# Attention stages of a three-layer block: where the compressed scores' step, the gates' tangents, two gate products and a rotary step stand in each engine's order

## The chip, the cores and the metric

The kernel runs on one core of a Trainium2 chip. The metric is the device time of one execution in microseconds (us). The program keeps five engines in step with semaphores: TensorE (PE; its weight loads are PEld) multiplies and transposes into eight PSUM banks of 128 x 512 fp32, ScalarE (ACT) copies, casts and evaluates functions, VectorE (DVE) does element-wise work and reductions, GpSimd (POOL) issues the DMAs of small tensors and some element-wise steps, and SyncE (SP) issues the weight loads.

## The reference

One sequence of 512 tokens, width 1024, passes through a first block and then through two equal layers, all in fp32. The first block is a gated feed-forward, a mixer and a second feed-forward. Its mixer has neighbourhood attention (8 heads, on an 8 x 64 grid) and three groups of dilated banded attention (4 heads each); both results are multiplied by sigmoid gates and summed. Each of the two layers mixes three attentions:

```python
o_a = nsa_attention(...)        # compressed + selected + window, 8 heads, 2 kv groups
o_b = swa_sink_attention(...)   # sliding window with sinks
o_c = mla_attention(...)        # latent: q and k = plain part (64) + rotated part (32)
g_a, g_b, g_c = jnp.split(jax.nn.sigmoid(h @ w_branch_gate), 3, axis=-1)
merged = g_a * (o_a @ w_branch_a) + g_b * (o_b @ w_branch_b) + g_c * (o_c @ w_branch_c)
x = x + merged @ w_out
```

In the compressed part a query sees 31 block summaries per kv group (held as 32), takes a masked softmax over them and multiplies by its own gate:

```python
s = einsum(qc, k_cmp) * scale
p_cmp = masked_softmax(s, cmp_end <= tq)
o_cmp = einsum(p_cmp, v_cmp)
```

## The kernel before

`Plan` writes a list of steps once; then each engine's program (`tensor`, `scalar`, `vector`, `gpsimd`, `sync`) walks the same list and issues its own part of each step in that order. So the place of a step in the list is its place in every engine's queue, and an engine whose next instruction waits holds up all that stands behind it. A semaphore value stands for all earlier instructions of its kind on that engine.

**Weights and products.** Every product is `dense` (L270): for each 128-row chunk three matmuls (L1691 to L1693; high and low parts of weights and activations), 24 of 128 x 512 for a full product of 1024 rows. A weight unit of 512 KB is loaded by SP (L2342), cast to its high part by ACT (L1877), and the rest is formed by DVE (L2010). `unit` asks for the split of the unit two ahead.

**PSUM.** Two rings of four banks: `PB`, taken in turn, and `OB`, which gives the bank that was given back longest ago. A bank is handed on with the events that must come before its next use.

**Attention** is `attend` (L508). Its input is a list of slots, each of two batches (two banks), taken two slots at a time as a pair. Turn p of the loop does, in this order: `turn` of the old pair (PE transposes the normalised scores of its four batches, L1775, and ACT copies each bank back, L1937); what waits in `behind`; `score` of the first new slot (PE L1767; DVE adds the mask and takes the extreme, L2083; ACT exponentiates, L1929) and of the second; `value` of the old slots (L1789); `norm` of the first new slot (DVE L2098 to L2114), `done` of the old, `norm` of the second new slot; then `between`: the hooks `post` and `pre` of the new units and a list of fill work, which keeps PE busy while DVE and ACT finish the softmax. A turn takes all four banks of `PB`, so the scores behind it wait until ACT has copied the first two.

**Fill work** is products for the gates. `gates` (L630) makes a whole product of 24 matmuls, whose bank `roomy` (L638) picks; `quarters` (L641) makes the same in four pieces of 6. `tangent` (L659) follows: DVE multiplies the bank by the norm's factor and so frees it (L2160), ACT takes the Tanh (L1953), and POOL stores the tile to DRAM (L2312). It runs at once when the bank is of `PB`, and in `behind`, after the next turn, when it is of `OB`. While four output banks are out or still to be opened `roomy` gives `PB`.

**Where the stages stand.** Neighbourhood attention: four pairs, fill `[ga[0:2], ga[2:3], ga[3:4], ga[4:6], ga[6:7]]`, the last list in the closing turn, which has no new scores. Its value tiles `va` come back from DRAM (`value_scratch`). Dilated groups 1 and 2: one pair each, fill of 8 and 4 quarters, right after the projections of their q and k. Latent attention (both layers): six pairs, fill `[opened[0:1], None, opened[1:2], None, opened[2:3], opened[3:4], opened[4:5]]`. Before pairs 1 and 3, `pre` calls `heads_in(2, True)` and `heads_in(3, True)`, which make the queries and keys of two more heads: three products for even m (plain keys, plain queries, rotated queries), two for odd. For even m ACT first copies the rotated bank (L1966), DVE multiplies it by the cosines (L2215), and the bank is free after both; then ACT copies the halves of the two plain banks (four of L1969). In the closing turn `done` of two output banks has been put in `behind` (ACT L1923, DVE L2076 free the bank).

Compressed, selected and window attention (both layers): eleven pairs, all fill in quarters. `post` of pairs 0, 2 and 5 issues `cmp_score` for the next query tile as one step, behind the norms of both slots: PE transposes two blocks (L1844), DVE masks, takes the maximum, subtracts (L2273, L2276, L2278), ACT exponentiates (L1997), and DVE, which waits for that, sums, inverts, weighs and multiplies (L2280 to L2286).

## Time and profile before

| | |
|---|---|
| median of 3 runs | 3093.63 us (3093.18 to 3093.67) |
| profiled execution, its own time | 3091.7 us |
| its span (first to last instruction) | 3089.5 us |
| PE busy | 3020.2 us |
| DVE busy | 1672.6 us |
| ACT busy | 1203.5 us |
| mean granted PE clock | 0.996 of full speed |

The chain of work that ended last is 89% PE. The span is the time between the first and the last instruction of the core; what the execution's own time has over it is start and end. Busy times are of instructions only, so 3089.5 less the busy time of an engine is the time in which it had nothing running.

### The profile page before, as it was taken

The page shows a single profiled execution, that of the slowest core. Times are in us where ns is not written, and L with a number is a line of the kernel's source. Part 1 is how long each engine was busy: PE and PEld are TensorE (multiplying, and loading weights), DVE is VectorE, ACT ScalarE, POOL GpSimd, SP SyncE. Part 2 cuts the span into 40 slices and gives each one's busy share as a digit, 9 for nine tenths or more (in the row PEclk, how much of TensorE's full clock was granted, in tenths as well). Part 3 has the DMA queues.
Part 4 walks back from the last instruction along what each step waited for, and adds up shares of the span by engine and source line. Part 5 has one row for each costly group of instructions (what it writes and reads, how often), then busy time and mean ns, then how long its engine had stood idle before and what let it go on. Part 6 is the DMA issues. An engine that isn't in the chain of part 4 may idle for free.

```text
span 3089.5 us, 40035 instructions
## 1 busy us (share of the span) xinstructions
PE 3020.2 (98%) x15272; PEld 2478.8 (80%) x15272; DVE 1672.6 (54%) x3050; ACT 1203.5 (39%) x2238; POOL 286.5 (9%) x344
## 2 busy tenths in 40 slices
PE   8999999999999999999999999999999999999998
PEld 7888887888888888778778888888778778888887
DVE  6653364446565426556656555436556666555434
ACT  4322334443432224645553322224546553322223
POOL 0000110001100012011001100013111001100002
PEclk9999999999999999999999999999999999999999
DMA  5333373325233333225225332334223315322332
GB/s 170 113 96 114 108 144 119 103 86 179 95 100 99 96 108 111 73 101 167 73 63 183 97 96 96 96 98 151 87 95 117 127 49 184 103 96 96 102 97 95
DMA packets 105996, 338.15 MB, mean 109 GB/s; under 512 B 15360, under 2 KB 15888, under 8 KB 105680
## 3 DMA queue, kind: packets, MB, share of 16 engines
q1 hardware_dynamic: 84816, 272.45, 28.0%
q0 software_dynamic: 20992, 63.15, 7.0%
q8 instruction: 123, 2.02, 0.3%
q14 instruction: 65, 0.53, 0.1%
HBM read 299.24 MB, written 27.52 MB: 106 GB/s over the span
## 4 chain that ended last, share of the span: by engine, by line
PE 89%; ACT 3%; DVE 3%; issue 2%; DMA 2%; POOL 1%; SPq 0%; POOLq 0%; DVEq 0%; ACTq 0%
PE bk L1691 26%; PE bk L1693 25%; PE bk L1692 25%; PE bk L1767 3%; PE bk L1789 3%; PE bk L1775 1%; PE bk L1730 1%; PE bk L1732 1%; PE bk L1731 1%; ACT t L1929 1%; ACT t L1937 1%; ACT t L1877 1%; DMA t<-value_scratch 0%; DVE t L2160 0%; DVE t L2010 0%
## 5 line engine op out<-in xcount | busy, mean ns | idle before, releaser
L1691 PE MATMUL bk<-t,t 128*128 128x512 f32 x3784 | 1481.0, 391 | 25.1 <-DVE t L2010 13.8
L1693 PE MATMUL bk<-t,t 128*128 128x512 f32 x3784 | 1469.2, 388 | 0.0
L1692 PE MATMUL bk<-t,t 128*128 128x512 f32 x3784 | 1468.3, 388 | 0.0
L1691 PEld LDWEIGHTS bk<-t,t 128*128 128x128 f32 x3784 | 712.6, 188 | 182.1 <-issue 26.2
L1693 PEld LDWEIGHTS bk<-t,t 128*128 128x128 f32 x3784 | 712.5, 188 | 147.3
L1692 PEld LDWEIGHTS bk<-t,t 128*128 128x128 f32 x3784 | 713.1, 188 | 141.9
L2010 DVE TENSOR_TENSOR t<-t,t 128x1024 fp32r<-128x1024 f32 (+3 forms) x538 | 616.7, 1165 | 353.9 <-ACT t L1877 353.2
L1877 ACT CAST t<-t 128x1024 fp32r<-128x1024 f32 (+3 forms) x538 | 511.3, 979 | 217.1 <-PE bk L1693 109.5
L1920 ACT CAST t<-t 128x512 fp32r<-128x512 f32 x88 | 54.6, 621 | 433.7 <-DVE t L2070 433.7
L1929 ACT ACTIVATE t<-t,t 128x256 f32<-128x256 f32 (+3 forms) x336 | 173.1, 516 | 95.8 <-DVE t L2083 94.9
L2316 POOL TENSOR_TENSOR t<-t,t 128x512 f32<-128x512 f32 x58 | 78.3, 1349 | 1387.4 <-ACT t L1907 1387.3
L2067 DVE SCALAR_TENSOR_TENSOR t<-bk,t 128x512 f32<-128x512 f32 x88 | 60.6, 691 | 246.8 <-PE bk L1693 246.7
L2083 DVE CUSTOM_DVE_ANT_0 t<-bk,t 128x256 f32<-128x256 f32 (+3 forms) x272 | 110.2, 456 | 125.3 <-PE bk L1767 77.9
L1903 ACT ACTIVATE t<-t,t 128x512 fp32r<-128x512 f32 x72 | 51.0, 722 | 224.3 <-DVE t L2293 195.1
L1767 PE MATMUL bk<-t,t 64*128 64x256 f32 (+7 forms) x672 | 115.3, 421 | 20.5 <-ACT t L1937 18.4
L1917 ACT ACTIVATE t<-t 128x512 f32<-128x512 f32 x88 | 55.5, 632 | 189.8 <-DVE t L2061 189.8
L1937 ACT COPY t<-bk 128x512 f32<-128x512 f32 (+2 forms) x200 | 95.3, 558 | 64.6 <-PE bk L1775 63.9
L1767 PEld LDWEIGHTS bk<-t,t 64*128 64x128 f32 (+1 forms) x672 | 65.7, 190 | 54.2 <-ACT t L1937 39.2
L2312 POOL DMA_DIRECT2D gate_scratch<-t x64 | 35.3, 552 | 728.1 <-ACT t L1953 563.4
L1789 PEld LDWEIGHTS bk<-t,t 128*64 128x64 f32 x1456 | 79.2, 137 | 24.3 <-issue 23.6
L1775 PE MATMUL bk<-t,t 128*128 128x128 f32 x728 | 90.6, 273 | 5.3 <-ACT t L1969 4.5
L1775 PEld LDWEIGHTS bk<-t,t 128*128 128x128 f32 x728 | 82.0, 140 | 15.4 <-ACT t L1969 5.7
(173 smaller groups left out, 1997.6 us busy)
## 6 DMA issues: line engine op xcount, KB each, us to landing
t<-in_f_g SPq DMA_DIRECT2D x88, 512.0 KB, 4.4
t<-in_f_u SPq DMA_DIRECT2D x88, 512.0 KB, 3.6
t<-in_f_d SPq DMA_DIRECT2D x64, 512.0 KB, 4.3
t<-in_gate SPq DMA_DIRECT2D x48, 512.0 KB, 3.7
gate_scratch<-t POOLq DMA_DIRECT2D x64, 256.0 KB, 2.3
t<-gate_scratch POOLq DMA_DIRECT2D x64, 256.0 KB, 3.7
t<-in_f_d SPq DMA_DIRECT2D x32, 384.0 KB, 3.1
t<-in_wo SPq DMA_DIRECT2D x24, 512.0 KB, 3.7
```

What stands on the lines that cost most here:

```text
L1691: pe.matmul(o, wh, xh, start=start, stop=False)
L1692: pe.matmul(o, wh, xl, start=False, stop=False)
L1693: return pe.matmul(o, wl, xh, start=False, stop=stop)
L1767: ins = pe.matmul(b["bank"][:, w["at"]:w["at"] + w["w"]], w["q"], w["k"], start=True, stop=True)
L1775: ins = pe.transpose(b["bank"][:, j * 128:(j + 1) * 128], b["S"][:, j * 128:(j + 1) * 128], P.cn("ident"))
L1789: ins = pe.matmul(v["o"], v["v"][j], b["PT"][:, c:c + 128], start=j == 0 and not v["add"], stop=end, skip_group_check=v["add"])
L1877: e.then_inc(act.copy(P.spl[u % NSPL][:, 0, 0:n], P.raw[u % NRAW][:, 0:n]), "halves", ("hi", u))
L1929: e.then_inc(act.activation(S, S, ACT.Exp, bias=w["nm"], scale=-1.0, accum_out=w["sm"]), "exps", (n, "e", j, i))
L1937: e.then_inc(act.copy(b["PT"][:, 0:b["w"]], b["bank"][:, 0:b["w"]]), "acts", (n, "a", j))
L2010: e.then_inc(dve.tensor_tensor(lo, P.raw[u % NRAW][:, 0:n], hi.bitcast(F32), ALU.subtract), "rests", ("lo", u))
L2083: e.then_inc(dve.tensor_tensor_reduce(b["S"][:, c:c + k], b["bank"][:, c:c + k], w["table"], -w["scale"], w["init"], ALU.add, ALU.min, w[" ...
L2316: e.then_inc(pool.tensor_tensor(P.acc[:], P.acc[:], s["q"][:], ALU.add), "pools", (n, "p"))
```

## The change

- **Compressed scores in two steps.** `cmp_score` keeps PE's transposes, DVE's first three operations and ACT's exponential. It is issued by a new hook `later`, between the norm of the first and of the second new slot. The four DVE operations behind the exponential become the step `cmp_share`, issued by `post` where all of it was before.
- **Tangents.** A gate product in `PB` inside `attend` still has its bank multiplied and freed at once; its Tanh and its store go to `behind`, so they follow the copies of the next turn.
- **Closing turn.** A flag `closing` makes `roomy` give `PB` in the closing turn. In latent attention this moves the fifth gate product from `OB` to `PB`.
- **Neighbourhood fill** becomes `[ga[0:3], ga[3:4], ga[4:5], ga[5:6], ga[6:7]]`: one product moves from turn 3 to turn 0.
- **Dilated groups 1 and 2.** A new argument `lead` issues the first quarter ahead of the first scores; the fill is then 7 and 4 quarters.
- **Latent heads.** In `heads_in(2, True)` the four copies of the plain banks come ahead of the rotated bank's copy and product.

```diff
@@ -172,6 +172,7 @@
         self.inside = False
+        self.closing = False
         self.unopened = 0
@@ -505,7 +506,7 @@
-    def attend(self, slots, fill=(), at_once=False):
+    def attend(self, slots, fill=(), at_once=False, lead=()):
@@ -513,6 +514,8 @@
         self.inside = True
+        for f in lead:
+            f()
@@ -579,17 +582,16 @@
+        def each(ss, name):
+            for s in ss:
+                for B in slots[s]:
+                    for U in B:
+                        if U.get(name):
+                            U[name]()
+
         def between(ss):
-            for f in ss:
-                for B in slots[f]:
-                    for U in B:
-                        if U.get("post"):
-                            U["post"]()
-            for f in ss:
-                for B in slots[f]:
-                    for U in B:
-                        if U.get("pre"):
-                            U["pre"]()
+            each(ss, "post")
+            each(ss, "pre")
             for f in next(fill, None) or ():
@@ -603,7 +605,9 @@
             if not new:
+                self.closing = True
                 between(())
+                self.closing = False
             for s in new[0:1]:
@@ -617,6 +621,7 @@
                 done(s)
+            each(new, "later")
             for s in new[1:2]:
@@ -636,14 +641,14 @@
     def roomy(self):
-        return self.OB if self.inside and len(self.OB.out) + self.unopened < 3 else self.PB
+        return self.OB if self.inside and not self.closing and len(self.OB.out) + self.unopened < 3 else self.PB
...
             if k == 0:
-                ring = self.roomy()
-                assert ring is self.OB
+                ring = self.OB
+                assert len(ring.out) < 3
                 b, bank, bt = ring.take()
@@ -657,16 +662,23 @@
     def tangent(self, name, m, ring, b, bank, tok):
-        def tangent():
+        def left():
             i, s, f = self.tmp.take()
...
             ring.give(b, (n, "g"))
-            self.gate_at[name, m] = (len(self.gate_at), self.load(self.D["gates"][len(self.gate_at)], s[:], (n, "t")))
-            self.tmp.give(i, self.gate_at[name, m][1])
+
+            def turned():
+                k = self.step("tangent", s=s, t=(n, "g"))
+                self.gate_at[name, m] = (len(self.gate_at), self.load(self.D["gates"][len(self.gate_at)], s[:], (k, "t")))
+                self.tmp.give(i, self.gate_at[name, m][1])
+            if self.inside and ring is self.PB:
+                self.behind.append(turned)
+            else:
+                turned()
         if ring is self.OB:
-            self.behind.append(tangent)
+            self.behind.append(left)
         else:
-            tangent()
+            left()
@@ -842,7 +854,7 @@
         self.unopened = 4
-        self.attend(self.batches(na_us), [ga[0:2], ga[2:3], ga[3:4], ga[4:6], ga[6:7]])
+        self.attend(self.batches(na_us), [ga[0:3], ga[3:4], ga[4:5], ga[5:6], ga[6:7]])
@@ -917,8 +929,8 @@
                     sms=dil_cols(S_SM, t, hh), rss=dil_cols(S_RS, t, hh), ot=lambda t=t, obk=obk: obk[t][2]))
-            self.attend(self.batches(us), self.portions(*[(gb[0:8], (3, 2, 2, 1)), (gb[8:20], (8, 4)),
-                                                          (gb[20:32], (8, 4))][g]), at_once=g > 0)
+            self.attend(self.batches(us), self.portions(*[(gb[0:8], (3, 2, 2, 1)), (gb[9:20], (7, 4)),
+                                                          (gb[21:32], (7, 4))][g]), at_once=g > 0, lead=[[], gb[8:9], gb[20:21]][g])
@@ -1231,7 +1243,7 @@
                     between()
-            if m % 2 == 0:
+            def turning():
                 places = to_place[m // 2] = []
@@ -1241,6 +1253,8 @@
                           done=rotated)
+            if m % 2 == 0 and not later:
+                turning()
             got = []
@@ -1251,6 +1265,8 @@
                 got.append((took, w))
+            if m % 2 == 0 and later:
+                turning()
             tq = got[1][0]
@@ -1492,6 +1508,11 @@
                         OB.give(b, (n, "b"))
+                        cmp_[qt] = (i, S, n)
+
+                    def cmp_shares(qt=qt):
+                        i, S, n = cmp_[qt]
+                        n = self.step("cmp_share", qt=qt, S=S, e=(n, "e"), sgs=sgs, sgt=sgt)
                         cmp_[qt] = (i, S, (n, "d"))
@@ -1514,14 +1535,18 @@
-                    def post(qt=qt, kind=kind, h=h, f_=cmp_scores, g_=cmp_turn):
+                    def post(qt=qt, kind=kind, h=h, f_=cmp_shares, g_=cmp_turn):
                         if h == 0 and kind == 0:
...
+                    def later(qt=qt, kind=kind, h=h, f_=cmp_scores):
+                        if h == 0 and kind == (qt > 0) and qt < 3:
+                            f_(qt + 1)
+
                     if qt == 0 and kind == 0 and h == 0:
-                        first_scores = cmp_scores
+                        first_scores = (cmp_scores, cmp_shares)
@@ -1540,10 +1565,11 @@
                                                        for j in range(qt + 1)],
-                        lambda: v_t, h, qt, 0.125, col, open=opn, post=post, done=done, most=4, add=True, gate=gate,
+                        lambda: v_t, h, qt, 0.125, col, open=opn, post=post, later=later, done=done, most=4, add=True, gate=gate,
                         sms=columns(S_SM, col, 1), rss=columns(S_RS, col, 1),
                         o=lambda qt=qt, h=h: half_out(obk[qt][1], h), ot=lambda qt=qt: obk[qt][2]))
-        first_scores()
+        for f in first_scores:
+            f()
         opened[14]()
@@ -1948,8 +1974,8 @@
                 e.then_inc(act.activation(a, a, ACT.Exp), "acts", (n, "a", g))
-        elif kind == "sigmoid":
-            e.wait_ge((n, "g"))
+        elif kind == "tangent":
+            e.wait_ge(s["t"])
             e.then_inc(act.activation(s["s"][:], s["s"][:], ACT.Tanh, scale=0.5), "acts", (n, "t"))
@@ -2267,8 +2293,7 @@
             mk = P.cn("cmpneg")[:, qt * 32:qt * 32 + 32].unsqueeze(1).broadcast_to([128, 8, 32])
-            some = P.cn("cmp01")[:, qt:qt + 1]
-            mx, sx = P.st[:, 168:176], P.st[:, 176:184]
+            mx = P.st[:, 168:176]
             e.wait_ge((n, "pe"), s["f"], P.c_tok)
@@ -2276,7 +2301,12 @@
             vec(dve.tensor_tensor(S3, S3, mx.unsqueeze(2).broadcast_to([128, 8, 32]), ALU.subtract), (n, "s"))
-            e.wait_ge((n, "e"))
+        elif kind == "cmp_share":
+            qt = s["qt"]
+            S3 = s["S"][:, 0:256].rearrange("p (h n) -> p h n", h=8)
+            some = P.cn("cmp01")[:, qt:qt + 1]
+            sx = P.st[:, 176:184]
+            e.wait_ge(s["e"])
             vec(dve.tensor_reduce(sx, S3, AX, ALU.add), (n, "1"))
```

## Rows read from the trace of the kernel before

**Rows 1.** The page, busy time of each engine: us, share of the span, instructions.

```profile
PE 3020.2 (98%) x15272; PEld 2478.8 (80%) x15272; DVE 1672.6 (54%) x3050; ACT 1203.5 (39%) x2238; POOL 286.5 (9%) x344
```

**Rows 2.** Waits of TensorE, whole span: us in total, times, longest us.

```profile
PE bk L1767 <- ACT t L1937: 18.4, 19, 3.2
...
PE bk L1691 <- ACT t L1923: 5.5, 2, 2.8
...
PE bk L1767 <- DVE t L2050: 1.5, 2, 0.7
```

**Rows 3.** The same view of 455:500, 1285:1318 and 1490:1560 us.

```profile
PE bk L1767 <- ACT t L1937: 2.3, 3, 0.8
...
PE bk L1767 <- ACT t L1937: 2.1, 3, 0.8
...
PE bk L1767 <- ACT t L1937: 5.4, 3, 3.2
```

**Rows 4.** Timeline, neighbourhood attention's first turn: start, length, idle before, releaser.

```profile
461.36 1.91 PE L1775 MATMUL bk<-t,t 128*128 128x128 f32 x16
464.02 2.11 PE L1767 MATMUL bk<-t,t 64*128 64x256 f32 x16 [0.75 <-ACT t L1937]
...
462.29 0.63 ACT L1953 ACTIVATE t<-t 128x512 f32<-128x512 f32 x1 [3.58 <-DVE t L2160]
```

**Rows 5.** Timeline, a turn with no tangent ahead of its copies.

```profile
1511.65 1.91 PE L1775 MATMUL bk<-t,t 128*128 128x128 f32 x16
1513.51 2.12 PE L1767 MATMUL bk<-t,t 64*128 64x256 f32 x16
...
1512.29 2.05 ACT L1937 COPY t<-bk 128x512 f32<-128x512 f32 x4 [1.72 <-PE bk L1775]
```

**Rows 6.** Timeline of TensorE, first value step of neighbourhood attention.

```profile
470.18 0.66 PE L1789 MATMUL bk<-t,t 128*64 128x128 f32 x8 [2.58 <-DMA t<-value_scratch]
```

**Rows 7.** Windows: length, busy time per engine, granted clock, DMA share, GB/s.

```profile
470.00:476.00 6.00, 5.83 (x24) 4.62 (x25) 2.73 (x8) 0.78 (x1) 0.00 (x0) 0.72 0.32 102
2198.00:2202.00 4.00, 3.95 (x10) 3.13 (x11) 1.69 (x1) 3.39 (x5) 1.28 (x1) 0.57 0.56 201
1499.70:1511.60 11.90, 11.89 (x84) 9.99 (x85) 7.30 (x30) 7.05 (x21) 0.54 (x1) 0.75 0.19 67
2452.40:2461.60 9.20, 9.19 (x84) 7.72 (x85) 7.33 (x30) 7.03 (x21) 0.54 (x1) 1.00 0.23 86
```

**Rows 8.** Timeline, latent attention's second turn, first such layer.

```profile
1276.54 0.63 PE L1775 MATMUL bk<-t,t 128*128 128x128 f32 x4 [1.39 <-ACT t L1969]
1277.78 1.06 PE L1775 MATMUL bk<-t,t 128*128 128x128 f32 x8 [0.60 <-ACT t L1969]
1278.92 2.94 PE L1767 MATMUL bk<-t,t 128*128 128x256 f32 x8
...
1272.53 0.61 ACT L1877 CAST t<-t 128x512 fp32r<-128x512 f32 x1
1274.76 0.58 ACT L1966 COPY t<-bk 128x512 f32<-128x512 f32 x1 [1.62 <-PE bk L1693]
1275.24 2.44 ACT L1969 ACTIVATE t<-bk 64x512 f32<-64x512 f32 x4
```

**Rows 9.** Timeline, compressed scores of the second query tile.

```profile
1494.64 1.91 PE L1775 MATMUL bk<-t,t 128*128 128x128 f32 x16
1499.71 2.93 PE L1767 MATMUL bk<-t,t 64*128 64x256 f32 x12 [3.16 <-ACT t L1937]
...
1493.47 0.69 DVE L2107 TENSOR_TENSOR t<-t,t 128x512 f32<-128x512 f32 x1
...
1495.76 0.41 DVE L2273 SCALAR_TENSOR_TENSOR t<-bk,t 128x256 f32<-128x256 f32 x1
...
1497.12 0.42 ACT L1997 ACTIVATE t<-t 128x256 f32<-128x256 f32 x1 [2.85 <-DVE t L2278]
...
1498.49 2.05 ACT L1937 COPY t<-bk 128x512 f32<-128x512 f32 x4
```

## The prediction

> **What bounds the kernel now.** I read the page first. TensorE is busy for 3020.2 of 3089.5 us [rows 1], so the kernel is a stream of matmuls with 69 us of holes, some 9 of them the start. No matmul is removed or added; the change can only close holes, open others, or move the clock. Then I read TensorE's waits. The largest group but the start is the scores (L1767) waiting for ACT's turn copies (L1937): 18.4 us in 19 pauses; then 5.5 us of gate products waiting for a bank that a split on ACT frees, and 1.5 us of scores waiting for a projected key [rows 2]. The same view by stage shows where: three pauses in neighbourhood attention (2.3 us), three in the later part of latent attention (2.1), three in compressed attention (5.4) [rows 3]. The two layers repeat each other's pauses, so a saving in the first is counted twice. Last I read the timeline around each pause, for what ACT did before its first copy, and the granted clock in windows.
>
> **The tangents.** At a turn TensorE transposes for 1.91 us. Where a `PB` gate product ends right ahead of it, ACT's next instruction is the Tanh, which must wait for DVE's product: it runs from 462.29 to 462.92, the copies follow, and the scores start 2.66 us after the turn (461.36 to 464.02), with 0.75 of idle time [rows 4]. Where no Tanh stands ahead, the first copy starts 0.64 us into the turn, four take 2.05, so the second is done some 1.7 us in, and the scores start 1.86 us after the turn with no pause [rows 5]. Moving the Tanh behind the copies makes the first case the second. That is worth all three pauses of neighbourhood attention, 2.3 us, and those of 1285 to 1318 us that have a Tanh ahead of them. There are three: 0.63, 0.73 and 0.75 by the timeline, 2.1 together [rows 3]. The 0.73 comes behind `heads_in(3)`, which is unchanged; two are left, 1.4 us, in each layer 1.4. What the Tanh now stands ahead of is the exponentials of the new scores. ACT has nothing then until DVE has read the scores, so one Tanh of 0.63 us is covered; three, behind the new first fill of neighbourhood attention, make 1.9 us, of which I take some 0.6 to delay the exponentials. The norms must be ready only after a further value step and a whole gate product, so this costs nothing; uncovered it would cost 0.6. The tiles in `tmp` and the stores go later by a turn, and nobody reads them before the merge.
>
> **The closing turn of latent attention.** The fifth gate product waits 2.77 us (5.5 in two times [rows 2]) because its `OB` bank is freed by a split that stands behind a Tanh and four copies on ACT. In `PB` it needs only the first copy, which now has no Tanh ahead. The first bank is copied while the turn still transposes [rows 5], so all 2.77 go, in each layer. The splits then run under the 24 matmuls. The bank is freed by DVE's product as before; the next stage needs it as its fourth.
>
> **One gate product moved to the first fill.** The value step waits 2.58 us for `value_scratch` [rows 6]. A gate product is 24 matmuls of the longest kind; at the mean of all PE instructions, 3020.2 / 15272 = 0.198 us [rows 1], they take at least 4.7 us, so with the 0.75 above gone TensorE comes to the value step 4.0 us later, behind the landing by 1.4. The moved split frees a weight buffer sooner, so a 512 KB weight load can run beside the value loads; it would have to delay them by more than 1.4 us to be seen. I take 2.58 in full; the bounds are 0 and 2.58. Turn 3 keeps one product as cover, as turns 1 and 2 have, and these have no pause for norms.
>
> **The clock.** After that pause the granted clock falls: 0.72 of full speed over the 6 us from 470 [rows 7], so (1 - 0.72) x 6 = 1.7 us lost between the 2.4 and the 1.2 GHz level. After the 3.16 us pause of compressed attention the same 84 PE instructions take 11.9 us at 0.75 in the first layer and 9.2 at 1.00 in the second [rows 7]: 2.7 us. I count both as given back, 4.4 together. The pause before 2198 us also has a fall behind it (0.57 over 4 us, 1.7 us) [rows 7]; that pause is in the initial `heads_in`, which is unchanged. The Trainium skill, "TensorE: Matmul & The Clock Gate", section "HAM oscillation — how this bites in real kernels", prices a fall as the throttled time x (1 - 1.2/2.4). By that rule the second fall, 11.9 us at a mean of 0.75, would cost 3.0 where the two layers differ by 2.7, and the whole sum would be 0.3 larger.
>
> **Compressed scores in halves.** Before, behind both norms, DVE runs three operations from 1495.76, ACT its exponential at 1497.12, then a cast, and only then the copies, at 1498.49, which the scores wait for until 1499.71 [rows 9]. The three DVE operations now start ahead of the second slot's norms. Those are two batches of some 1.05 us (the multiplication alone 0.69 [rows 9]) and the small copy of `cmp_turn`, 0.4, so ACT's exponential, cast and copies come 2.5 to 2.7 us sooner: copies from 1495.8, the second done by 1496.9. In turn DVE norms the second slot 1.3 us later (1495.76 to 1497.1 is what the three take), so the turn, which was all transposed at 1496.55, ends some 0.5 later. The scores start at about 1497.15 instead of 1499.71: 2.6 of 3.16. The bounds are 1.9 (the whole 1.3 is seen) and 3.16. At the other two places the pauses are 5.4 - 3.16 = 2.2 together [rows 3]. The turn starts there with the norms done long enough ahead, so I take 2.2 in full; bounds 0.9 and 2.2. Per layer 4.8. DVE's backlog then moves: the shares, a weight rest and a gate's product stand ahead of the next peaks, about 1 to 1.8 us late against TensorE. Covers are the waits of DVE for the value step that frees the score tiles, and the quarters of fill.
>
> **Latent heads.** The turn now waits 1.39 for the key bank and 0.60 for the query bank, whose copies ACT makes behind the rotated bank's; ACT itself stands idle for 1.62 us, until the third product is done [rows 8]. Put first, the four plain copies can start when the cast ends, at 1273.14, and end 2.44 later, at 1275.6; the rotated copy follows to 1276.15, and its product of 0.7 frees the bank at about 1276.9. The turn's last four transposes then end at 1277.4 and the scores start at about 1277.5 instead of 1278.92: 1.4. The bounds are 0.6 (just the order of one 0.58 us copy) and 2.0. The swap's DMAs start 0.9 us later on SP, and the next weight load behind them too; the rotated rows are wanted a turn later.
>
> **The lead quarter.** Six matmuls (at least 1.2 us by the same mean) fill the 0.73 us for which the scores wait for the key, twice: 1.5 [rows 2]. Its split moves ahead of the peaks on DVE, which costs them about 0.2; the first fill is 7 quarters instead of 8 and still longer than the softmax.
>
> **The sum.** Neighbourhood 2.3 + 2.6; lead 1.5; latent 2 x (1.4 + 2.8 + 1.4) = 11.2; compressed 2 x 4.8 = 9.6; clock 4.4. Together 31.6 us. The profiled execution took 3091.7, so 3060.1; the median of the runs is 1.9 above that execution, so 3093.6 - 31.6 = **3062**.
>
> **Rivals.**
> - *The backlog on DVE is seen.* The late norms of the second slot hold up the turn at each of the six places, by up to the three operations' 1.3 us, and the peaks behind them: 6 x 1.3 = 8 us back, 3070. For it: in compressed attention DVE has the shares, rests and norms in a row. Against: DVE is busy for 7.3 of 9.2 us there [rows 7].
> - *The clock falls elsewhere.* The 3.16 us pause is there in both layers and had a fall behind it in one only [rows 7]. The pause of the initial `heads_in` stays in both layers; one or two falls more, or none of the 4.4 given back, is 3064 to 3068. The skill's same page (section "What's actually happening") has the clock follow how busy the array has been lately, and its moment vary from run to run; by that a fall at 470 or 1500 is not sure to go, which is this rival.
> - *Half of it is not there.* The value loads land later with the weight load beside them, and the second halves of the exchange cost as much as they give: none of 2.6 + 1.7 at neighbourhood attention, 0.6 instead of 1.4 at the heads, 0.9 for 2.2: about 3071.
> - *Slower.* One mechanism: the first half of the scores, put between the norms, holds the turn so long that each of six places has a new 3.16 us pause, with 1.3 more and a fall of 2.7 behind it: 6 x 7.2 = 43, less the 13.5 that pauses and fall cost there already, is +29.7; the other stages save 19.3; net +10, 3104. It decides when a place costs above (19.3 + 13.5) / 6 = 5.5 us. The norms would have to be over 4 us late, and they are delayed by 1.3.
> - *No effect.* Each hole is followed by another wait of its own length; for that every one of five separate edits would have to fail.
>
> **Chances.** Forecast, 3058 to 3066: 0.62. DVE's backlog, to 3070: 0.13. Clock, to 3068: 0.12. Half, to 3074: 0.07. No effect 0.03, slower 0.02, still less than 3058: 0.01. The range that leaves out no more than 2 in 10 is 3058 to 3071. A change of 0.2% is 6.2 us, about what a measurement of this kernel can tell from none; faster by more has 0.95, within it 0.03, slower 0.02.
>
> **What would show it.** Right: scores behind L1937 wait under 5 us in all instead of 18.4; no wait for `value_scratch`; no L1691 wait for L1923; the key wait of L2050 gone; granted clock 1.00 near 475 and 1500. A wait of the turn (L1775) for DVE's norms in compressed attention would be the first rival, windows under 0.9 behind short pauses the second. Wrong by much: a pause of over 2 us at any place that had none, or peaks (L2083) so late that quarters end before the norms.

## The result, and the profile after

The changed kernel took 3057.69 us (median of 4 runs, 3057.0 to 3058.85), the kernel before 3093.4 beside it (4 runs, 3092.82 to 3093.67): a ratio of 0.9885, 95% interval 0.9868 to 0.9902, 35.7 us saved. The forecast was 3062 with a range of 3058 to 3071: the direction and the case were right, the gain was 4.1 us larger than the 31.6 of the sum, and the time lies 0.3 us below the range, on the side to which the forecast had given a chance of 0.01: all its rivals made the time longer. The profiled execution took 3057.74 us with a span of 3055.6. One execution of the kernel before, beside the experiments below, took 4685.77 us at a mean granted clock of 0.604, and no ratio or mean below counts it.

The page's row of TensorE's busy time, and its waits over the whole span (us in total, times, longest), which answer to [rows 1] and [rows 2]:

```profile
PE 3013.4 (99%) x15272; PEld 2474.4 (81%) x15272; DVE 1669.0 (55%) x3050; ACT 1204.0 (39%) x2238; POOL 289.1 (9%) x344
...
PE bk L1717 <- ACT t L1995: 3.6, 2, 1.8
...
PE bk L1793 <- ACT t L1963: 2.6, 6, 0.7
...
PE bk L1801 <- DVE t L2241: 1.5, 2, 0.8
...
PE bk L1801 <- DVE t L2319: 1.3, 2, 0.6
PE bk L1829 <- DVE t L2177: 1.0, 1, 1.0
```

The lines have moved: scores are L1793 (before L1767), the turn's transposes L1801 (L1775), their copies L1963 (L1937), dense matmuls L1717 to L1719 (L1691 to L1693), the tangent L1979 (L1953), a head's plain copies L1995 (L1969). The scores' wait for the copies fell from 18.4 us in 19 pauses to 2.6 in 6. The waits for the split (5.5), for the projected key (1.5) and for `value_scratch` (2.6) are not in the list any more. TensorE's pauses of 0.15 us and more were 60 with 60.3 us and are 41 with 33.0.

The windows behind the old pauses, and behind the one that stayed (the numbers behind the busy times are the granted clock, the DMA share and GB/s), to be held against [rows 7]:

```profile
470.00:476.00 6.00, 6.00 (x58) 4.88 (x55) 4.39 (x23) 6.00 (x22) 1.67 (x3) 1.00 0.53 195
1477.90:1489.40 11.50, 10.77 (x99) 8.82 (x98) 10.83 (x39) 9.46 (x31) 0.54 (x1) 1.00 0.21 70
2175.00:2179.00 4.00, 3.71 (x11) 2.96 (x12) 1.47 (x1) 3.61 (x6) 1.45 (x2) 0.64 0.65 201
2401.70:2413.20 11.50, 11.01 (x89) 8.51 (x78) 7.62 (x30) 6.46 (x22) 1.12 (x2) 1.00 0.31 103
```

The clock stays full at 470 us and in both compressed stages. Ahead of the final stores it fell in one place only, behind the 1.82 us pause of the initial `heads_in`, which the change leaves alone.

The timeline at neighbourhood attention's first turn (start, length, then idle time before and its releaser), to be held against [rows 4]:

```profile
467.85 1.91 PE L1801 MATMUL bk<-t,t 128*128 128x128 f32 x16
...
468.48 2.05 ACT L1963 COPY t<-bk 128x512 f32<-128x512 f32 x4 [9.93 <-PE bk L1801]
...
469.70 2.12 PE L1793 MATMUL bk<-t,t 64*128 64x256 f32 x16
470.39 1.70 ACT L1979 ACTIVATE t<-t 128x512 f32<-128x512 f32 x3
...
471.74 1.97 PE L1815 MATMUL bk<-t,t 128*64 128x128 f32 x32
...
471.96 0.53 ACT L1955 ACTIVATE t<-t,t 128x256 f32<-128x256 f32 x1
```

The copies start 0.63 us into the turn, and the scores 1.85 us behind it instead of 2.66, as forecast by [rows 5]. The three tangents stand behind the copies, and the first exponential starts where they end. The value step follows the scores without the 2.58 us of [rows 6].

Latent attention's closing turn:

```profile
1312.76 1.60 PE L1801 MATMUL bk<-t,t 128*128 128x128 f32 x12
1314.12 0.48 PE L1717 MATMUL bk<-t,t 128*128 128x512 f32 x1
...
1314.44 0.39 PE L1718 MATMUL bk<-t,t 128*128 128x512 f32 x1
...
1314.67 0.39 PE L1719 MATMUL bk<-t,t 128*128 128x512 f32 x1
...
1313.18 1.81 ACT L1963 COPY t<-bk 128x256 f32<-128x256 f32 x4 [3.47 <-PE bk L1801]
1314.89 1.08 ACT L1949 CAST t<-bk 128x512 fp32r<-128x512 f32 x2
```

The gate product (L1717) follows the transposes at once, and the split (L1949), which it waited for, runs under it. From the turn to the value step are 7.0 us (1312.76 to 1319.77) instead of 10.0 (1324.90 to 1334.91 in the kernel before).

Latent attention's second turn, to be held against [rows 8]:

```profile
1265.60 1.65 PE L1801 MATMUL bk<-t,t 128*128 128x128 f32 x12
1268.01 0.63 PE L1801 MATMUL bk<-t,t 128*128 128x128 f32 x4 [0.75 <-DVE t L2241]
1268.47 0.81 PE L1793 MATMUL bk<-t,t 128*128 128x256 f32 x3
...
1264.08 2.45 ACT L1995 ACTIVATE t<-bk 64x512 f32<-64x512 f32 x4
1266.55 0.59 ACT L1992 COPY t<-bk 128x512 f32<-128x512 f32 x1
```

One pause of 0.75 us stands in place of 1.39 and 0.60, and it is the one foretold: for DVE's product, which frees the rotated bank.

The compressed scores of the second query tile, to be held against [rows 9]:

```profile
1479.25 1.77 PE L1801 MATMUL bk<-t,t 128*128 128x128 f32 x12
1481.65 0.65 PE L1801 MATMUL bk<-t,t 128*128 128x128 f32 x4 [0.63 <-DVE t L2319]
1482.23 1.13 PE L1793 MATMUL bk<-t,t 64*128 64x256 f32 x8
...
1479.27 0.42 ACT L2023 ACTIVATE t<-t 128x256 f32<-128x256 f32 x1 [0.17 <-DVE t L2303]
1479.59 1.03 ACT L1903 CAST t<-t 128x1024 fp32r<-128x1024 f32 x1
1480.64 2.28 ACT L1963 COPY t<-bk 128x512 f32<-128x512 f32 x4
...
1480.57 0.69 DVE L2133 TENSOR_TENSOR t<-t,t 128x512 f32<-128x512 f32 x1
1481.17 0.42 DVE L2319 COPY t<-bk 128x256 f32<-128x256 f32 x1
```

From the turn to the scores are 2.98 us instead of 5.07. What is left is another wait than the one removed: the turn's last four transposes need the `PB` bank that `cmp_turn` holds, and DVE's small copy of it (L2319) now stands behind the second slot's norms (L2133).

### The profile page after: what moved, and what is told of

It reads as the page before. It is cut to its first block, busy times and chain, and to the rows that moved or that the text cites. A ratio compares the mean times of both kernels' runs of the same rounds, so it can differ in the third digit from the quotient of the medians.

```text
span 3055.6 us, 40040 instructions
## 1 busy us (share of the span) xinstructions
PE 3013.4 (99%) x15272; PEld 2474.4 (81%) x15272; DVE 1669.0 (55%) x3050; ACT 1204.0 (39%) x2238; POOL 289.1 (9%) x344
## 4 chain that ended last, share of the span: by engine, by line
PE 91%; ACT 3%; DVE 2%; issue 2%; DMA 1%; POOL 1%; SPq 0%; POOLq 0%; DVEq 0%; ACTq 0%
PE bk L1717 26%; PE bk L1719 26%; PE bk L1718 26%; PE bk L1793 3%; PE bk L1815 3%; PE bk L1801 2%; PE bk L1756 1%; PE bk L1757 1%; PE bk L1758 1%; ACT t L1955 1%; DVE t L2036 0%; ACT t L1903 0%; PE bk L1769 0%; DMA t<-gate_scratch 0%; ACT t L1995 0%
## 5 line engine op out<-in xcount | busy, mean ns | idle before, releaser
L1717 PE MATMUL bk<-t,t 128*128 128x512 f32 x3784 | 1480.2, 391 | 19.6 <-DVE t L2036 14.6
L1719 PE MATMUL bk<-t,t 128*128 128x512 f32 x3784 | 1468.6, 388 | 0.0
L1717 PEld LDWEIGHTS bk<-t,t 128*128 128x128 f32 x3784 | 712.3, 188 | 175.6 <-issue 26.9
L1719 PEld LDWEIGHTS bk<-t,t 128*128 128x128 f32 x3784 | 712.4, 188 | 146.9
L1963 ACT COPY t<-bk 128x512 f32<-128x512 f32 (+2 forms) x200 | 96.7, 559 | 103.1 <-PE bk L1801 102.0
L1793 PE MATMUL bk<-t,t 64*128 64x256 f32 (+7 forms) x672 | 112.7, 414 | 3.2 <-ACT t L1963 2.6
L1801 PE MATMUL bk<-t,t 128*128 128x128 f32 x728 | 91.4, 273 | 4.2 <-DVE t L2241 1.5
L1801 PEld LDWEIGHTS bk<-t,t 128*128 128x128 f32 x728 | 82.0, 140 | 15.1 <-issue 3.2
L1793 PEld LDWEIGHTS bk<-t,t 64*128 64x128 f32 (+1 forms) x672 | 64.1, 187 | 35.2 <-ACT t L1963 22.0
```

What stands on the lines that cost most here:

```text
L1717: pe.matmul(o, wh, xh, start=start, stop=False)
L1719: return pe.matmul(o, wl, xh, start=False, stop=stop)
L1793: ins = pe.matmul(b["bank"][:, w["at"]:w["at"] + w["w"]], w["q"], w["k"], start=True, stop=True)
L1801: ins = pe.transpose(b["bank"][:, j * 128:(j + 1) * 128], b["S"][:, j * 128:(j + 1) * 128], P.cn("ident"))
L1963: e.then_inc(act.copy(b["PT"][:, 0:b["w"]], b["bank"][:, 0:b["w"]]), "acts", (n, "a", j))
```

## The experiments

**How executions are compared.** The kernel before, run many times beside the experiments, took from 3088 to 3101 us (71 executions), more than most single edits are worth. A profile tells why. Windows of 2 us over the whole span give the granted clock in each; (1 - clock) x 2, summed over all windows but the last 16 us (the final stores), is the time lost to the clock. It comes in portions of 1.7 us, one or two behind a pause, and "remainder" below is the span less that. The places are the starts of these windows, "x2" a double portion. The sum counts the whole time of a fall, also what of it lies inside the pause: the double fall of 1498 began at 1498.81 and the scores at 1499.71, so it is priced 0.45 us too high (3.4 for 3.0).

| kernel | span | the clock fell at | lost | remainder |
|---|---|---|---|---|
| before | 3089.5 | 470, 1498 x2, 2198 | 6.8 | 3082.7 |
| before_again | 3089.2 | 1328, 1498, 2278, 2476 | 6.8 | 3082.4 |
| before_third | 3092.8 | 470, 1526, 2198, 2280 x2, 2454 | 10.3 | 3082.5 |
| changed | 3055.6 | 2176 | 1.7 | 3053.9 |
| after_again | 3053.8 | nowhere | 0 | 3053.8 |
| only_split | 3077.5 | 1328, 2270 x2 | 5.1 | 3072.4 |
| only_tangents | 3088.9 | 472, 706, 1328, 1498, 2226, 2276, 2448, 2474 | 13.7 | 3075.2 |
| only_closing | 3083.2 | 1246, 2222, 2444 | 5.1 | 3078.1 |
| only_fill | 3089.6 | 702, 1246, 1328 x2, 1502, 2228 | 10.2 | 3079.4 |
| only_lead | 3088.4 | 470, 1246, 1326, 2446 x2 | 8.5 | 3079.9 |
| only_heads | 3087.7 | 472, 1328, 1500, 2278, 2448 | 8.5 | 3079.2 |
| whole_at_later | 3090.7 | 472, 1332, 1502, 2450 | 6.8 | 3083.9 |
| key_ahead | 3051.9 | nowhere | 0 | 3051.9 |
| plain_ahead_all | 3049.7 | nowhere | 0 | 3049.7 |
| key_ahead_other_bank | 3050.4 | nowhere | 0 | 3050.4 |
| plain_other_bank | 3049.6 | nowhere | 0 | 3049.6 |

**before_again, before_third and after_again: is the spread the clock?** The two kernels, unchanged.

> The kernel before, unchanged, profiled once more. Theory (executions differ by the number of times that the granted clock falls to half behind a pause, and each fall takes 1.7 us; the schedule itself costs 3082.7 us in every execution, the 3089.5 of its profile less four times 1.7): the profile shows a number n of falls at places of about 472, 706, 1248, 1330, 1502, 2200 to 2228, 2278 and 2450, and the span is 3082.7 plus 1.7 n within 1 us, whatever n is. Rival (the executions differ by the length of the pauses themselves, a transfer that is now and then late): the span less 1.7 n is off by more than 2 us.

> The kernel before, unchanged, a third profile, for the same question: span 3082.7 plus 1.7 n within 1 us by the theory, with n likely 3 to 6 and not at the same places as in the other two.

> The changed kernel, unchanged, in more executions beside kernel before. Theory: its span is 3053.9 plus 1.7 n with n of 0 to 2, since only two or three places are left behind which the clock fell in any run, so its times spread over 3 to 4 us (3056 to 3060) where those of before spread over 9. Rival (the few falls of its first profile were chance): times up to 3065.

They took 3091.3 and 3094.93 us; windows of the first and then of the second:

```profile
470.00:476.00 6.00, 5.71 (x31) 4.69 (x31) 3.16 (x10) 1.24 (x3) 0.00 (x0) 1.00 0.29 93
1326.00:1332.00 6.00, 4.11 (x12) 3.33 (x13) 2.51 (x3) 2.50 (x5) 0.14 (x1) 0.76 0.28 93
...
2198.00:2202.00 4.00, 4.00 (x19) 3.29 (x18) 3.34 (x5) 3.76 (x6) 1.21 (x1) 1.00 0.44 144
```

```profile
1326.00:1332.00 6.00, 3.23 (x19) 2.48 (x18) 2.84 (x4) 4.06 (x8) 0.54 (x1) 1.00 0.20 79
...
2196.00:2202.00 6.00, 4.58 (x13) 3.64 (x14) 3.00 (x3) 4.88 (x9) 2.54 (x2) 0.72 0.42 134
2278.00:2286.00 8.00, 5.23 (x15) 4.05 (x15) 2.51 (x3) 3.87 (x8) 0.54 (x1) 0.66 0.30 99
```

The fall behind 470 us, on which the forecast counted, is missing in the first of them and one at 1326 is there instead; in the second it is the other way round, and behind 2278 there is a double one. The remainders of three profiles are 3082.7, 3082.4 and 3082.5, those of the changed kernel 3053.9 and 3053.8. So by these profiles the schedule's own gain is 28.7 us, and the rest of the difference between two executions is mostly the number of falls. The changed kernel's times in the repeat (median 3057.7, 3055.89 to 3058.91, 4 runs; ratio 0.9884, 0.9865 to 0.9902) stay within 3.0 us of each other, those of the kernel before within 13 (3088.08 to 3101.22, 7 runs). Both rivals fell.

A place at which the clock fell looks like this (before_again, TensorE's timeline; its window is the second one above):

```profile
1327.89 0.47 PE L1691 MATMUL bk<-t,t 128*128 128x512 f32 x1 [2.77 <-ACT t L1923]
```

**Each part alone.** Each of these is the kernel before with one part of the change's diff. only_split has `cmp_share`, `later` and what calls them; only_tangents the new `tangent`; the other four are

```diff
# only_closing (and the flag, set around the last `between`)
-        return self.OB if self.inside and len(self.OB.out) + self.unopened < 3 else self.PB
+        return self.OB if self.inside and not self.closing and len(self.OB.out) + self.unopened < 3 else self.PB
# only_fill
-[ga[0:2], ga[2:3], ga[3:4], ga[4:6], ga[6:7]]
+[ga[0:3], ga[3:4], ga[4:5], ga[5:6], ga[6:7]]
# only_lead (lines shortened)
-(gb[8:20], (8, 4)), (gb[20:32], (8, 4))
+(gb[9:20], (7, 4)), (gb[21:32], (7, 4)), lead=[[], gb[8:9], gb[20:21]][g]
# only_heads: the rotated copy behind the plain ones
+            if m % 2 == 0 and later:
+                turning()
```

> The kernel before with the compressed scores in two steps and nothing else. Theory (a pause costs its idle time plus the overlap that matmuls lose at a stop, some 0.1 us): per layer 3.16, 1.63 and 0.62 us of waiting for the turn copies shrink to one wait of about 0.6, 4.8 + 0.2 us, and the fall of the clock behind 1500 us goes, 2.7: 12 to 13 us less than before, about 3081. Rival (the clock falls elsewhere instead): 10 us, 3083.5, with a granted clock under 0.9 in some window where before had 1.00.

> The kernel before with the tangents of PB gates behind the next copies and nothing else. Theory: the turn-to-scores time falls from 2.66 to 1.86 us where a Tanh stood ahead. In neighbourhood attention the first 0.8 is given to the wait for value_scratch, which grows from 2.6 to 3.4; the two others give 1.6, the stage's end 0.6 to 1.1; in each layer 1.6 and some 0.6 of the closing turn's 2.77. Together 6.5 to 7.5 us, about 3086.5. Rival (the whole of every idle time and no more): 2.3 + 2 x 1.4 = 5.1 us, 3088.3.

> The kernel before with PB for the closing turn's gate and nothing else. The product now waits for the first turn copy, which still stands behind a Tanh: it starts 1.9 us into the turn plus 0.2 instead of 4.4, so each layer gives 2.3 to 2.6 us, 4.6 to 5.2 together, about 3088.5. Rival (the bank taken from PB is missed by the value step or the next stage): a new wait of the next products, under 3 us in all.

> The kernel before with the neighbourhood fill of 3, 1, 1, 1, 1 products and nothing else. Theory: the wait for value_scratch (2.58) goes whole and takes the clock's fall behind it along (1.7); with the overlap 4.3 to 4.7 us, about 3089. Rivals: the fall comes all the same, behind another pause, 2.7 us, 3090.7; or the weight load beside the value loads delays them, and a wait for value_scratch stays.

> The kernel before with the lead quarters of dilated groups 1 and 2 and nothing else. By the recorded sum 1.5 us (the 0.73 us waits of the scores for the key, twice). If a pause also costs the overlap of the matmuls around it, 1.9 to 2.1: 3091.4 against 3091.9.

> The kernel before with the plain copies ahead of the rotated one in the third head set, nothing else. Sum on record: 1.4 per layer, 2.8. With the overlap 3.0: about 3090.4. In the trace: waits of the turn for L1969 copies gone there, one of about 0.75 for the rotated bank's product in their place.

Against the kernel before on the same chips (medians 3093.76 for the first four, 3092.97 for the other two, from some 29 runs each), and with the remainder against the 3082.5 of the kernel before:

| kernel | median (runs) | ratio, 95% interval | remainder less by | the forecast's terms, without clock |
|---|---|---|---|---|
| only_split | 3079.70 (5) | 0.9960, 0.9948 to 0.9972 | 10.1 | 9.6 |
| only_tangents | 3087.11 (12) | 0.9980, 0.9971 to 0.9988 | 7.3 | 5.1 |
| only_closing | 3085.37 (11) | 0.9977, 0.9968 to 0.9985 | 4.4 | 5.5 |
| only_fill | 3090.73 (11) | 0.9991, 0.9982 to 0.9999 | 3.1 | 2.6 |
| only_lead | 3092.25 (12) | 0.9996, 0.9987 to 1.0004 | 2.6 | 1.5 |
| only_heads | 3092.53 (11) | 0.9997, 0.9989 to 1.0006 | 3.3 | 2.8 |

Five of the parts give what the sum's terms said within 1.1 us, where the waits ahead of the first matmuls alone differ by 0.5 to 1 us between executions; no part is worth nothing. only_tangents gives 2.2 more, as its expectation said (6.5 to 7.5): it also shortens each closing turn's pause, from 2.77 to 1.94 us, and the stage's end. The medians tell that badly: only_lead and only_heads save 2.6 and 3.3 us of schedule and 0.7 and 0.4 us of median, because falls take it back. only_fill came out at its rival's 3090.7 and not at the 3089 of its theory: the fall at 470 us was gone from its profile, and six portions at other places stood there instead.

Every execution, profiled or not, has its own mean granted clock, known to three digits. Span times this clock is a remainder with the falls in the final stores taken out too. Its mean is 3078.9 us for the 71 executions of the kernel before and 3048.7 for the eight of the changed kernel. Against the kernel before on their own chips the parts, in the table's order, come to 10.0, 7.5, 4.5, 2.4, 3.0 and 4.1 us less (standard errors of 0.3 to 0.8). The clock took 13.9 us from only_lead on average and 15.2 from only_heads, against 12.1 from the kernel before beside them.

The six remainders of the table add up to 30.8, the whole change's is 28.7. The parts share a pause, as the waits of only_tangents over the whole span show:

```profile
PE bk L1774 <- ACT t L1944: 13.5, 12, 3.2
...
PE bk L1796 <- DMA t<-value_scratch: 4.4, 1, 4.4
PE bk L1698 <- ACT t L1930: 3.9, 2, 1.9
```

The gate product's wait for the split (L1930) falls from 5.5 to 3.9 there, since the tangents' move shortens what stands ahead of that split; only_closing takes it away too. The value step waits 4.4 us instead of 2.6: the turn ends sooner and the values land a little later, so a pause closed ahead of that landing gives nothing until the moved product covers it. Of the 1.8 us more, 0.8 are the earlier turn; the landing itself moves from execution to execution, since in kernels that are alike up to there the wait was 2.2 to 3.4 us.

**whole_at_later: do the halves matter?** The compressed step at its new place, between the norms of the first and of the second new slot, but in one piece:

```diff
+            for s in new:
+                for B in slots[s]:
+                    for U in B:
+                        if U.get("later"):
+                            U["later"]()
# cmp_scores, unsplit, is called by "later" instead of "post"
```

> The kernel before with the compressed scores' step moved whole between the norms, not split: DVE waits there for ACT's exponential and runs the four last operations ahead of the second slot's norms, which come 3.2 us later than before instead of 1.3. Theory (both the place and the split count): the turn's last banks wait for the norms for about as long as the scores waited for the copies; 0 to 2 us less than before, 2.7 more if the clock keeps up. Rival (the place alone does it): as only_split, 12 us.

It took 3091.66 us (3087.28 to 3092.67, 11 runs), 0.9993 of the kernel before (0.9985 to 1.0002); its remainder is 1.4 us longer, 0.8 of it a longer wait for `value_scratch` (3.4 us for 2.6), and over all its runs the mean remainder is 0.2 us shorter. Its waits over the whole span, and its timeline at the first place:

```profile
PE bk L1774 <- ACT t L1944: 7.6, 13, 0.8
PE bk L1782 <- DVE t L2105: 7.4, 8, 2.0
```

```profile
1498.09 1.03 PE L1782 MATMUL bk<-t,t 128*128 128x128 f32 x8
1501.08 0.63 PE L1782 MATMUL bk<-t,t 128*128 128x128 f32 x4 [1.96 <-DVE t L2105]
```

The scores' wait for the copies is gone (18.4 to 7.6), and the turn's wait for the norms (L2105) has come in its place: DVE waits for the exponential and makes the four operations of the shares before it norms the second slot. This is the backlog rival's mechanism, and with the step in one piece it eats the whole gain. The halves are worth 3083.9 - 3072.4 = 11.5 us by the two profiles, and 9.8 by the means of all runs (10.0 less 0.2).

**What is left.** From the changed kernel, in `heads_in` with `later` unset: key_ahead makes the key's copies ahead of the rotated copy, plain_ahead_all all four plain ones; the bank's edit is

```diff
-                         b, bank2, bt = PB.take()
+                         b, bank2, bt = OB.take()
...
-                        PB.give(b, (n, "d"))
+                        OB.give(b, (n, "d"))
```

> All of the changed kernel, and in each head's step the key's two plain copies also stand ahead of the rotated copy on ScalarE. Theory (every pause on TensorE costs its length and the overlap of the matmuls around it, and the 1.82 us pause at 2175 us, or what is around it, brings the clock down): the pauses of 1.82 us in front of the dilated layers' scores shrink in both layers, about 1.9 us each, and the clock behind 2175 us stays at full, about 1.7 us more: 3052. Rival (the wait there is for the rotated rows, which come later by the two copies): the pause stays as a wait on VectorE, and the time is 3057 to 3059.

> All of the changed kernel, and all four plain copies ahead of the rotated one in the same step. Theory: the first pause closes, but the chain copy, product on VectorE, sum, placed rows starts about 2.4 us later and opens a pause of 1.5 to 2 us at the scores behind it, so 3056 to 3058, about the changed kernel's time. Rival (the placed rows have slack enough): 3052.

> The kernel of key_ahead, and the compressed step's turn takes its bank from the other pool, so that the next turn's last bank isn't held by it. Theory (the 0.63 us pause ahead of the compressed layer's first scores is for that bank's copy on VectorE): that pause closes, about 0.5 to 0.6 us in each of two layers, so 1 us below key_ahead: 3051. Rival (the other pool's bank is then late for a value product): same as key_ahead within 0.5 us.

> All four plain copies ahead, and the compressed step's turn in the other pool's bank. By adding what each gave in its own run (2.2 us less than key_ahead from the plain copies, 1.5 us less than key_ahead from the bank, both with the clock's falls taken out): a span of 3048.2 and a time of 3050.3, and no fall of the clock before the tail. Rival (the bank's 1.5 us came from elsewhere): 3051.8, as plain_ahead_all.

key_ahead took 3053.99 us (0.9868 of the kernel before, 0.9854 to 0.9883), plain_ahead_all 3051.84 (0.9864, 0.9847 to 0.9880), key_ahead_other_bank 3054.94 (0.9870, 0.9856 to 0.9885), each in 4 runs beside 3094.32; plain_other_bank 3051.82 (0.9867, 0.9846 to 0.9889) beside 3093.42. TensorE and ScalarE of plain_ahead_all around the place where the changed kernel had its 1.82 us pause:

```profile
1243.93 2.84 PE L1791 MATMUL bk<-t,t 128*128 128x128 f32 x12
...
1233.64 2.45 ACT L1993 ACTIVATE t<-bk 64x512 f32<-64x512 f32 x4
1236.11 0.59 ACT L1990 COPY t<-bk 128x512 f32<-128x512 f32 x1
```

The plain copies now run while ScalarE used to stand idle ahead of the rotated copy, the pause is closed, and the scores behind it (L1791) start without a wait (in the second layer after 0.43 us): my theory of a new pause of 1.5 to 2 us fell, its rival held. key_ahead left a wait of 0.93 us at those scores, for DVE's copies of rotated rows (L2254), so only half of the 1.9 us that I expected there came back. The other bank:

```profile
1477.50 1.76 PE L1801 MATMUL bk<-t,t 128*128 128x128 f32 x12
1479.65 0.63 PE L1801 MATMUL bk<-t,t 128*128 128x128 f32 x4 [0.39 <-DVE t L2133]
```

The turn's wait of 0.63 us becomes one of 0.39 for the norms themselves: about 0.25 us a layer, not the 0.5 to 0.6 that I expected. The remainders of single profiles hide part of what the bank is worth, since the first matmuls did not start alike: TensorE's 31st instruction came at 19.17 us in key_ahead and 18.83 in key_ahead_other_bank, at 19.05 in plain_ahead_all and 19.64 in plain_other_bank. From there to the last products the other bank saved 1.2 us in the first pair and 0.7 in the second, 0.5 of it at the two pauses; the rest is spread over small waits. The medians show nothing of it (3053.99 and 3054.94, 3051.84 and 3051.82). plain_ahead_all is, with plain_other_bank, the fastest that was run: 5.9 us less than the changed kernel, 4.2 of them by the remainders, and the rest is about one portion of the clock.

## Why the prediction was right on the pauses, and where it failed

By stage, from the start of the same matmul in the two profiles, with the clock's portions taken out:

| term | forecast | measured |
|---|---|---|
| neighbourhood: tangents and moved product | 4.9 | 6.2 |
| lead quarter | 1.5 | 2.0 |
| latent attention, each layer | 5.6 | 6.2, 6.2 |
| compressed attention, each layer | 4.8 | 4.2, 4.5 |
| clock, between the two profiles | 4.4 | 5.1 |
| clock, from profile to median | 0 | 1.8 |
| start and end of the execution | 0 | -0.7 |

The rows between and the rounding leave 0.2 of the 35.7 over.

- **The bound and the holes.** Right. TensorE was the stream with holes, each named pause closed, and no wait over 2 us came at a new place.
- **Tangents.** Right: 1.85 us from turn to scores, nothing lost at the exponentials or norms. Not counted in the forecast were two pauses at the end of neighbourhood attention (of 0.2 and 0.8 us, closed or shortened), 1.1 us: the term took the pauses of one window and stopped ahead of the stage's close.
- **Closing turn.** Right: 3.0 us for 2.77.
- **Heads.** Right: 1.5 us for 1.4, with the foretold pause.
- **Lead.** 2.0 for 1.5. A pause costs its listed idle time and the overlap of the matmuls on either side. In a stream without pauses a matmul of 0.39 us starts 0.23 us behind its forerunner (1314.44 and 1314.67 above), that is, before the forerunner's listed end; the listed idle time counts from that end. So each closed pause gave 0.05 to 0.25 us more than its row. That is most of latent attention's 0.6 a layer too.
- **Compressed.** 4.2 and 4.5 for 4.8: at the first place 2.1 of 3.16 came back and not 2.6, as I had DVE's small copy of `cmp_turn` in the sum of work ahead but not what is held until it is done, the turn's last bank. The 0.5 us for late norms, taken for the whole, came as this wait.
- **The clock.** This step failed. "I count both as given back, 4.4 together" took the falls of one execution for the kernel's own, and the sum then carried the 1.9 us between profile and median over as if the changed kernel had it too. Three profiles of the kernel before have falls at three different sets of places, 6.8, 6.8 and 10.3 us together. Its median time, 3093.4, less the 2.2 us between span and time and the 3082.5, leaves 8.7 us, five portions; the changed kernel's median leaves 3057.69 - 2.1 - 3053.9 = 1.7, one. So 7.0 us of the 35.7 are the clock's, where the forecast had 4.4, and the schedule's 28.7 stand against 27.2. These two, 2.6 and 1.5, are the miss. The 1.9 us was itself about one more portion of the clock. How the 35.7 divide is known only to some 1.5 us, though. By span times mean clock of all executions the schedule gave 30.2 and the clock 5.4, so that the clock's term is short by 1.0 and the schedule's by 3.0. One reason is the start: TensorE's 31st instruction came at 19.7 and 19.2 us in the two profiles of the changed kernel and at 18.6 to 19.1 in the three of the kernel before, ahead of everything that was changed, and the stages alone gave 29.3 (the table). By either reckoning both terms were too small, and the rest of the schedule's miss is the pauses and the overlap named above.
- **Rivals.** DVE's backlog is true of the unsplit step and not of the halves. "The clock falls elsewhere" was right as a mechanism and had the wrong sign here: it reckoned with fewer falls given back, never with more. "No effect" speaks of five separate edits; there are six. A fall moves between places from one execution to the next, but each of them stands behind a pause, and the long pauses are gone. The Trainium skill, "TensorE: Matmul & The Clock Gate", section "What's actually happening", says that the same kernel shows a different number of slow matmuls from run to run, which it says of a kernel's start; the traces show it in the middle of a kernel too (four, four and six portions). Its section "HAM oscillation — how this bites in real kernels" prices a fall at half of the throttled time. The remainders agree: with that price three profiles whose spans differ by 3.6 us come to within 0.3.

A count of pauses would have brought the clock's term nearer. Between start and end the kernel before has eleven pauses of over 1.3 us (those of 470, 1247, 1276, 1329, 1499, 1526 us and the second layer's five), and the changed kernel has two, of 1.82. The one profile that the forecast had lost four portions at eleven such pauses, and nine pauses fewer, at 4 / 11 of a portion each and 1.7 us a portion, are 5.6 us. The three profiles, two of them taken later, lost 14 portions at 33 such pauses, which makes it 6.5. Both are estimates; 7.0 or 5.4 were measured.

The length counts too. In the sixteen profiles together 30 of the 45 pauses of 1.9 us and more had a fall behind them, or beginning in them, 13 of the 59 between 1.3 and 1.9 us, one of the 18 between 0.95 and 1.3, and none of some 290 between 0.6 and 0.95. The change closed all five long ones. Five falls were double, and they are the five that began 0.7 to 1.1 us before their pause ended; of the 39 single ones the earliest began 0.64 us before that, and most began behind it.

Open: what decides at which of these pauses the clock falls in a given execution, and when. The shortest with a fall behind it had 1.11 us (only_tangents, at 706); the changed kernel's pause at 698 us has 1.0 and had none.

## What to carry to other kernels

When executions of one kernel differ by more than the edit is worth, take the time lost to the granted clock out of each profile and compare what is left: here that left 0.3 us between profiles whose spans differed by 3.6. Then hold it against the mean clock of every execution, since one profile's remainder was off by up to 1.6 us (whole_at_later). Forecast the clock from how many pauses remain that could bring a fall, and how long they are, not from the falls that one profile shows. When a step is moved ahead on an in-order engine, move only the half that someone waits for, and list what each instruction behind it holds (a bank, not only its output).

## What the runs showed of the hardware

- Each fall of the clock ahead of the final stores began behind a pause of 1.1 to 4.4 us or inside it, but only 12 of the 33 pauses over 1.3 us in the three profiles of the kernel before had one, and not the same in each execution. Of pauses of 1.9 us and more two in three had one (30 of 45, in sixteen profiles), of those between 1.3 and 1.9 us two in nine (13 of 59). A fall cost 1.7 us or twice that, and between none and eight portions were lost in one profiled execution of 3.1 ms.
- A single edit that closes short pauses does not make falls fewer for sure: over its 11 executions only_heads lost 15.2 us to the clock on average, the final stores included, against 12.1 in the kernel before beside it and 6.9 in the changed kernel.
- With the 1.82 us pauses shortened to 0.9 or closed, four kernels' profiles in a row showed the full clock up to the final stores. Their other executions were not profiled, and key_ahead_other_bank's took 1.7 to 3.6 us longer than the profiled one, so falls are not excluded there.
